# Gathering the tokens of eight experts at once instead of four, in a one-core diffusion step with a mixture of experts

## The reference, cut to what matters

```python
hid = silu(einsum('nd,edf->nef', xt, w_gate)) * einsum('nd,edf->nef', xt, w_up)   # D = 1024, F = 512
hid = hid * gates[..., None]                                                       # zero but for 2 of 16 experts
y = einsum('nef,efd->nd', hid, w_down)
```

## Time and profile before

| | |
|---|---|
| median of 3 runs | 787.18 us (785.57 to 787.45) |
| profiled execution, its time | 786.11 us |
| its span in the trace | 784.2 us |
| TensorE busy | 759.6 us, 97% of the span |
| VectorE, ScalarE, GpSimd busy | 356.6, 160.4 and 58.2 us |
| granted TensorE clock, mean | 0.995 of full speed |
| read from HBM | 286.31 MB, 368 GB/s over the span |

### The profile page before, as it was taken

One profiled execution on the slowest core, in us unless ns is written; L12 is line 12 of the kernel. 1 busy time (PEld: TensorE's weight loads), 2 busy tenths in 40 slices (PEclk: granted clock), 3 DMA queues, 4 the chain that ended last, 5 costly groups with the idle time before them and its releaser, 6 DMA issues.

```text
span 784.2 us, 11547 instructions
## 1 busy us (share of the span) xinstructions
PE 759.6 (97%) x4960; PEld 410.0 (52%) x4967; DVE 356.6 (45%) x560; ACT 160.4 (20%) x368; POOL 58.2 (7%) x70
## 2 busy tenths in 40 slices
PE   6999999999999999999899999999999999999987
PEld 5655646886434443444245546788643444344424
DVE  0206899786422232132248956788732223213222
ACT  3111224504112111120021111460411211112002
POOL 0410052001100000000010005200110000000000
PEclk8999999999999999999999999999999999999999
DMA  8999699898999999999999970679979999999993
GB/s 313 369 357 409 237 386 410 315 390 327 426 409 427 426 419 424 424 420 425 421 398 401 387 287 8 250 286 393 387 303 399 427 426 419 424 427 417 425 421 148
DMA packets 52980, 289.45 MB, mean 369 GB/s; under 512 B 3448, under 2 KB 5808, under 8 KB 27840
## 3 DMA queue, kind: packets, MB, share of 16 engines
q1 hardware_dynamic: 51200, 285.30, 90.4%
q0 software_dynamic: 1488, 3.31, 1.3%
q10 hardware_dynamic: 240, 0.08, 0.0%
HBM read 286.31 MB, written 2.37 MB: 368 GB/s over the span
## 4 chain that ended last, share of the span: by engine, by line
PE 77%; DMA 12%; DVE 5%; SPq 3%; issue 2%; ACT 1%; POOL 0%; DVEq 0%; ACTq 0%
PE ps L1236 23%; PE ps L879 12%; PE ps L1266 12%; PE ps L1150 7%; DMA ring<-in_w_e_up 5%; PE ps L1220 4%; DMA ring<-in_w_e_down 4%; DMA ring<-in_w_mod 3%; PE ps L897 3%; PE ps L1281 2%; SPq L635 1%; PE ps L727 1%; DVE pT L1860 1%; PE ps L1248 1%; PE ps L1028 1%
## 5 line engine op out<-in xcount | busy, mean ns | idle before, releaser
L1236 PE MATMUL ps<-ring,xe 128*64 128x512 f32 x688 | 151.6, 594 | 4.2 <-DMA ring<-in_w_e_up 4.2
L879 PE MATMUL ps<-ring,hT 128*128 128x512 f32 (+1 forms) x320 | 125.7, 551 | 0.0
L1236 PEld LDWEIGHTS ps<-ring,xe 128*64 128x64 f32 x688 | 48.6, 137 | 105.1 <-issue 100.6
L2205 DVE COPY ye<-ps 64x512 f32<-64x512 f32 (+1 forms) x28 | 19.3, 689 | 163.7 <-PE ps L1266 163.5
L1266 PE MATMUL ps<-ring,exhid 128*32 128x512 f32 x736 | 92.3, 594 | 0.8 <-DMA ring<-in_w_e_down 0.6
L879 PEld LDWEIGHTS ps<-ring,hT 128*128 128x128 f32 x320 | 60.1, 190 | 60.7 <-issue 58.4
L1150 PE MATMUL ps<-hT,ring 128*128 128x256 f32 x256 | 57.1, 381 | 0.0
L2189 DVE RECIPROCAL exhid<-exhid 128x512 f32<-128x512 f32 x16 | 53.6, 3353 | 0.5
L2187 DVE TENSOR_SCALAR exhid<-exhid 128x512 f32<-128x512 f32 x16 | 6.8, 427 | 103.2 <-ACT exhid L1678 103.2
L1266 PEld LDWEIGHTS ps<-ring,exhid 128*32 128x32 f32 x736 | 26.0, 110 | 53.0 <-issue 49.4
L1150 PEld LDWEIGHTS ps<-hT,ring 128*128 128x128 f32 x256 | 48.0, 190 | 7.4 <-issue 1.0
(11 more groups left out here) (294 smaller groups left out, 867.0 us busy)
## 6 DMA issues: line engine op xcount, KB each, us to landing
ring<-in_w_mod SPq DMA_DIRECT2D x24, 2048.0 KB, 16.8
ring<-in_w_e_up SPq DMA_DIRECT2D x23, 2048.0 KB, 19.9
ring<-in_w_e_gate SPq DMA_DIRECT2D x20, 2048.0 KB, 22.8
ring<-in_w_e_down SPq DMA_DIRECT2D x19, 2048.0 KB, 23.1
beside<-in_w_e_gate SPq DMA_DIRECT2D x8, 2048.0 KB, 22.1
ring<-in_w_in SPq DMA_DIRECT2D x7, 2048.0 KB, 20.4
beside<-in_w_e_down SPq DMA_DIRECT2D x7, 2048.0 KB, 20.3
beside<-in_w_e_up SPq DMA_DIRECT2D x5, 2048.0 KB, 18.6
```

What stands on the lines that cost most here:

```text
L879: mm = pe.matmul(bank[:, 0:width], hT[:, k, b * P:(b + 1) * P], w[:, k, :], start=(k == 0), stop=(k == KD - 1))
L1236: mm = pe.matmul(bank[PLACES * j:PLACES * j + PLACES, :], xe[:, k, c:c + PLACES], w[:, j, i, :], start=(k == 0), stop=(k == KD - 1))
L2205: ins = dve.tensor_copy(ye[r, plane, 512:1024], bank[r, :])
```

## The change

The tokens of eight experts are gathered at once, with 256 columns per product, ahead of pair 0 and inside pair 3. There is a second place for gathered tokens: `xe` holds the first four experts of a half, and a new tile `small` the other four. `small` is shared with the mixer's small tiles, so ScalarE and VectorE wait for the stores of the state before they write it, and the columns of ones are written again in each layer. A bank now holds one block of 128 features for eight experts, and is copied out by two instructions, on ScalarE for even blocks and on VectorE for odd ones. `count` moves to bank 6.

```diff
@@ bank_plan
-        put(("count", l), 5)
-        for i, bank in enumerate((0, 3, 1, 2)):
-            put((("gather", 0, i), l), bank)
+        for k in range(KD):
+            put((("gather", 0, k), l), (0, 3, 4, 5)[k % 4])
+        put(("count", l), 6)
...
-            if pair % 2 == 1 and pair < PAIRS - 1:
-                for i in range(4):
-                    put((("gather", pair // 2 + 1, i), l), i % 2)
+            if pair == PAIRS // 2 - 1:
+                for k in range(KD):
+                    put((("gather", 1, k), l), k % 2)
@@ build
-        C0 = sb("C0", [P, 2 * MH, MD + 1])
...
+        small = sb("small", [P, KD * 4 * PLACES])
...
+        C0 = share(2 * MH * (MD + 1)).rearrange("p (g e) -> p g e", g=2 * MH)
...
+        places = (xe, small[:, :].rearrange("p (k c) -> p k c", k=KD))
@@ TensorE
-                def gather(q, *which):
-
-                    for i in which:
-                        bank = begin((("gather", q, i), l))
-                        for k in range(2):
-                            for b in range(NB):
-                                c = b * TOK + k * P
-                                mm = pe.matmul(bank[:, c:c + P], htok[:, b, 2 * i + k, :],
-                                               pick[:, b, 4 * q:4 * q + 4, :].rearrange("p e c -> p (e c)"), start=True, stop=True)
-                        done((("gather", q, i), l), mm)
+                def gather(h, *which):
+
+                    for k in which:
+                        bank = begin((("gather", h, k), l))
+                        for b in range(NB):
+                            mm = pe.matmul(bank[:, b * 2 * P:(b + 1) * 2 * P], htok[:, b, k, :],
+                                           pick[:, b, 8 * h:8 * h + 8, :].rearrange("p e c -> p (e c)"), start=True, stop=True)
+                        done((("gather", h, k), l), mm)
...
-                    refill = p % 2 == 1 and q + 1 < QUADS
+                    refill = p == PAIRS // 2 - 1
...
-                        gather(q + 1, 0, 1)
+                        gather(1, 0, 1, 2, 3)
                     turn_hidden(p)
...
-                        gather(q + 1, 2, 3)
+                        gather(1, 4, 5, 6, 7)
...
-                gather(0, 0, 1, 2, 3)
+                gather(0, *range(KD))
@@ ScalarE
+                def pick_out(h, *which):
+
+                    for k in which:
+                        key = (("gather", h, k), l)
+                        bank = full(act, key)[:, :].rearrange("p (b q e s) -> p q b e s", b=NB, q=2, e=4)
+                        for q in range(2):
+                            ins = act.activation(places[q][:, k, :].rearrange("p (e b s) -> p b e s", e=4, b=NB), bank[:, q], ACT.Copy)
+                        ins.then_inc(free(key), 1)
...
-                pick_out(0, 0, 1, 2, 3)
+                act.wait_ge(state_out, 16 * STATE_OUTS * (l + 1))
+                pick_out(0, 0, 2, 4, 6)
@@ VectorE
-            dve.memset(vx[:, :, :, HD:], 1.0)
-            dve.memset(cv[:, :, HD:], 1.0)
...
                 normalise(l)
                 dve.memset(mv[:, :, :, MD:MD + 1], 1.0)
+                dve.memset(vx[:, :, :, HD:], 1.0)
+                dve.memset(cv[:, :, HD:], 1.0)
...
-                chosen(0, 4).then_inc(pick_ready, 1)
+                chosen(0, 8).then_inc(pick_ready, 1)
...
-                chosen(4, E).then_inc(pick_ready, 1)
+                chosen(8, E).then_inc(pick_ready, 1)
...
+                dve.wait_ge(state_out, 16 * STATE_OUTS * (l + 1))
+                pick_out(0, 1, 3, 5, 7)
                 modulation_columns(*last_section(l))
...
+                    if refill:
+                        pick_out(1, 1, 3, 5, 7)
```

More of the change, by code:

```diff
@@ L318, in build, with share @@
         m0 = sb("m0", [64, DEPTH, NB])
-        C0 = sb("C0", [P, 2 * MH, MD + 1])
[L320 to L326, removed]
+        small = sb("small", [P, KD * 4 * PLACES])
+        took = [0]
+        def share(n):
+            took[0] += n
+            return small[:, took[0] - n:took[0]]
+        C0 = share(2 * MH * (MD + 1)).rearrange("p (g e) -> p g e", g=2 * MH)
+        ck = share(NKV * HD)
+        cv = share(NKV * (HD + 1)).rearrange("p (g d) -> p g d", g=NKV)
+        vx = share(NB * NKV * (HD + 1)).rearrange("p (b g d) -> p b g d", b=NB, g=NKV)
+        rstd = share(TOK)
+        qc = share(NB * 4 * 8).rearrange("p (b q g) -> p b q g", b=NB, q=4)
+        qk_r = share(NB * (NQ + NKV)).rearrange("p (b h) -> p b h", b=NB)
+        peaks = share(NB * NQ).rearrange("p (b h) -> p b h", b=NB)
+        hr = share(NB * MH).rearrange("p (b h) -> p b h", b=NB)
+        nst = share(P)[0:8, :]
         shares = sb("shares", [P, NB, NQ])
         dn = sb("dn", [P, NB, MH, 2])
-        hr = sb("hr", [P, NB, MH])
-        nst = sb("nst", [8, P])
         mnew = sb("mnew", [64, DEPTH])
@@ L1210, in _ @@
                 token_rows(3)
-                warm((("scat", 0), l), 3)
-                def gather(q, *which):
-                    for i in which:
-                        bank = begin((("gather", q, i), l))
-                        for k in range(2):
-                            for b in range(NB):
-                                c = b * TOK + k * P
-                                mm = pe.matmul(bank[:, c:c + P], htok[:, b, 2 * i + k, :],
-                                               pick[:, b, 4 * q:4 * q + 4, :].rearrange("p e c -> p (e c)"), start=True, stop=True)
-                        done((("gather", q, i), l), mm)
+                warm((("gather", 0, 2), l), 3)
+                def gather(h, *which):
[5 more added lines that the diff above has]
+                        done((("gather", h, k), l), mm)
                 def into_hidden(p, u):
@@ L1231, in into_hidden @@
                             k = KD // 2 * part + i
-                            if p % 2 == 0 and u == 0 and k % 2 == 0:
-                                taken(pe, (("gather", p // 2, k // 2), l))
+                            if p % 4 == 0 and u == 0:
+                                taken(pe, (("gather", p // 4, k), l))
                             for j in range(2):
                                 c = (p % 2 * 2 + j) * PLACES
-                                mm = pe.matmul(bank[PLACES * j:PLACES * j + PLACES, :], xe[:, k, c:c + PLACES], w[:, j, i, :],
+                                mm = pe.matmul(bank[PLACES * j:PLACES * j + PLACES, :], places[p // 2 % 2][:, k, c:c + PLACES], w[:, j, i, :],
                                                start=(k == 0), stop=(k == KD - 1))
@@ L1665, in _ @@
                 token_copy(3)
[L1667 to L1672, removed]
+                def pick_out(h, *which):
[5 more added lines that the diff above has]
+                        ins.then_inc(free(key), 1)
                 def pair(p):
-                    q, a = p // 2, p % 2
-                    refill = a == 1 and q + 1 < QUADS
+                    refill = p == PAIRS // 2 - 1
                     bank = full(act, (("gate", p), l))
@@ L1684, in pair @@
                     if refill:
-                        pick_out(q + 1, 0, 1)
+                        pick_out(1, 0, 2)
                     key = (("turn", p), l)
@@ L1689, in pair @@
                     if refill:
-                        pick_out(q + 1, 2, 3)
+                        pick_out(1, 4, 6)
                     key = (("down", p, 0), l)
@@ L2176, in _, with pick_out @@
                 dve.tensor_tensor(beb(R_G), beb(R_W), per_col(r(R_X, 6, 8), E), ALU.mult).then_inc(gates_ready, 1)
+                def pick_out(h, *which):
+                    for k in which:
+                        key = (("gather", h, k), l)
+                        bank = full(dve, key)[:, :].rearrange("p (b q e s) -> p q b e s", b=NB, q=2, e=4)
+                        for q in range(2):
+                            ins = dve.tensor_copy(places[q][:, k, :].rearrange("p (e b s) -> p b e s", e=4, b=NB), bank[:, q])
+                        ins.then_inc(free(key), 1)
+                dve.wait_ge(state_out, 16 * STATE_OUTS * (l + 1))
+                pick_out(0, 1, 3, 5, 7)
                 modulation_columns(*last_section(l))
```

## The result

The kernel after takes 795.63 us (median of 4 runs, 795.25 to 796.65), the kernel before 787.09 us in the same comparison: 1.0114 times as long, 95% interval 1.0097 to 1.0132. The forecast was 793.1 us in a range from 789.5 to 796.5 us: slower, as said, but by 2.5 us more, and above the forecast's own range of 791.3 to 794.9 us. By the medians the change costs 8.5 us. The profiled execution took 795.25 us with a span of 793.3 us, 9.1 us more than before.

The account below looks back on a forecast made before the run. The prediction took the weight stream, held back by the first gather, as the bound. Two layers at +3.25 us took the profiled 786.11 us to 792.6; adjusted for run spread, 793.1 us, own range 791.3 to 794.9, with rivals 789.5 to 796.5.

Parts of the forecast that it names:

- Reading of the profile: Expert stages: the gapless weight stream behind the first gather sets their end, at 422 and 420 GB/s, despite TensorE's 97%.
- First gather: Ahead of pair 0 in each layer: 16 products of 256 columns take 7.06 us for 3.81, so 3.25 us more.
- rival that prices a product by the instruction: First gather: wide instructions cost 119 ns like narrow ones, so it stays 3.81 us; no change, 786.6 us; 6%.
- It passes on in full: From first gather to stage end: the whole 3.25 us delay reaches the end of each layer, 2 x 3.25 = +6.5 us.
- Layer 0: Transfers have some stock at 204.88 us, none at 225.38 us; the 0.3 us gap there grows by 3.25 us.
- rival by which layer 0 hides the delay: Queue at 225.38 us holds more, so layer 0's stream ends as before, +0.9 us there; 790.8 us; 10%.
- Copies: Two per bank on ScalarE and VectorE, 1.77 us per bank against 2.65 us available: they fit and cost nothing.
- `chosen`: Ahead of the gather: eight experts take about 0.2 us more, covered by ScalarE's last copy; cost nothing, uncovered 0.2 us per layer.
- waits for the state: New `state_out` waits of ScalarE and VectorE ahead of pair 0: already over when reached, because GpSimd passes the same wait; nothing.
- late banks: Rival at the first gather: PSUM banks come back late, 1.1 us more per layer, 795.3 us; 8%.
- Pairs 1 and 5: A gather vanishes from each: some 1.8 us saved of 3.8, the rest becoming TensorE waits for VectorE and ScalarE.
- rival that TensorE's total sets the end: Expert stages: two gathers of 7.06 us replace four of about 3.8, 1.0 us less per layer; 784.5 us; 6%.

Follow-up runs that it names:

- third experiment: Changed kernel with only four experts gathered ahead of pair 0, the next four in pair 1, 32 unused products in pair 5: 786.52 us, 0.9991 of the kernel before.
- fourth experiment: Kernel before plus four extra 512-column products between `count` and the first expert product, in each layer: 795.24 us, ratio 1.0106.
- first experiment: Changed kernel plus 64 unused 16-column products per layer (128 instructions) where TensorE waits in pairs 1 and 5: 793.6 us, 1.0078 of the kernel before.
- fifth experiment: Changed kernel plus 64 unused products (128 instructions) at the very front: 791.95 us, 1.0064 of the kernel before.
- second: Kernel before plus 64 unused 16-column products (128 instructions) at the front, where TensorE waits for its first weights: 790.0 us, ratio 1.0038.
- sixth experiment: Kernel before plus 128 unused products (256 instructions) at the front: 788.29 us, ratio 1.0023.
- seventh experiment: Changed kernel with only two experts gathered ahead of pair 0, two in pair 0, four in pair 1, the rest wide in pair 3: 791.7 us, 1.0065 of before.
- eighth experiment: Changed kernel with the same two-expert first gather, and `count` moved behind the first expert product: 792.52 us, 1.0067 of the kernel before.

## Why the prediction was right, and where it was not

**Reading of the profile.** Right: TensorE's 97% said nothing, the stream of weights behind the first gather did. The third and fourth experiments are the two halves of the proof: take the growth away and the time is back, add only a delay and the time is lost. The waits for weights that are left in pair 7 of the kernel after, and those of the fourth experiment, say that it is the stream and not TensorE's sum.

**First gather.** 3.25 us more were forecast, 7.14 - 3.81 = 3.33 and 7.15 - 3.81 = 3.34 us measured; the price by rows 7 held. The rival that prices a product by the instruction is refuted at 256 columns: there the rows, and not the figures of the Trainium skill (TensorE: Matmul & The Clock Gate, Back-to-back issue gap), decide. At 64 and 128 columns, though, the seventh experiment shows a price by the instruction, 118 ns for 64 columns and 119 ns for 128.

**It passes on in full.** That was somewhat too much. Stages of the three kernels with the wide first gather (after, first and fifth experiment) are longer than before by 2.42, 3.07, 3.12 us in layer 0 and 2.09, 2.83, 2.40 us in layer 1, a mean of 2.66. Stages of the kernels whose first gather is as before (second, third and sixth experiment) differ from it by -0.96 to +0.33 us, a mean of -0.36; such is the scatter of one profile each. So some 2.7 to 3.0 us of 3.33 arrive per layer, 5.3 to 6.0 us for the forecast's 6.5. By the clock, the first and fifth experiments are 5.4 to 6.8 us slower than the kernel before on the same chip, the fifth with a 0.65 us stall at its end. What takes the rest up is open, but for a part of layer 1: there the last down product waited 0.61 us for its weights in the kernel before, and in the kernel after it does not.

**Layer 0.** The sum was right, its place was not. The prediction gave the queue some stock at 204.88 us and put the growth at 225.38 us. The windows show the larger hole at 208 to 212 us, right behind the late first issue, and a smaller one at 230 to 232. The rival by which layer 0 hides the delay has fallen with it.

**Copies, `chosen`, waits for the state, banks.** Costed at nothing, and the third experiment, which leaves the shared memory and ScalarE's wait in, agrees; VectorE's copies and its wait are judged by the start of the first expert product alone. In the kernel after the first expert product starts 0.35 us (`count`) after the gather's end, and the 32 instructions of the gather take 7.14 us for the 7.06 of the earlier trace rows; late banks are not to be seen.

**Pairs 1 and 5.** Right. From the up product's end (242.86 us) to the down product 2.41 us, where it was about 4.2: 1.8 us saved of 3.8. In the first experiment's pair 1 the 32 unused products fit into the rest without a delay (2.29 us).

**The rival that TensorE's total sets the end**, 784.5 us: refuted for the kernel after. It has 121 records of TensorE fewer, and its stages end later with TensorE waiting for weights in pair 7, 1.23 us at the last block in both layers. But the margin is thin: in the seventh and eighth experiments TensorE's own sum does reach the end.

**The missing term.** The step that failed is the sum: it let the change act only through its work, and had no term for where the code lies. In the trace the stall and the lower clock behind it lengthen the step into layer 1 by 4.37 us. By the clock, counted from the kernel before in each comparison, moving the code at the front (fifth experiment) takes off 3.1 us (8.5 less 5.4), and that kernel still has its own stall of 0.65 us at the end; the first experiment takes off 1.7 us (8.5 less 6.8), where the intervals of the ratios reach 1.4 us (after) and 1.8 us to either side. So 5.3 to 6.0 us of gather and about 2 to 4 us of stall make up the 8.5 us, and the forecast of 6.5 us came close to the first and had nothing for the second. That the range held the time is luck: it reached so high for the late banks (795.3 us), which turned out to cost nothing.

## What to carry to other kernels

Look for the wait at which a full buffer is first given back: work ahead of the first product that reads such a buffer is paid nearly in full (2.7 to 3.0 of 3.33 us per layer here). The same work later is free only as long as the engine still waits for transfers at the end, 2.1 and 2.7 us here, and these waits are soon used up. Widening a product saves little where its price goes by the column (223 ns for 256 columns, 119 ns for 128) and narrowing it nothing where it goes by the instruction (118 ns for 64 columns), so measure both ends in the kernel's own trace. When a kernel's time moves by some us that no wait explains, look for "issue" gaps behind branches, and move the code (here by 128 instructions) before the change is blamed.

## What was not expected of the hardware

**Code that comes late.** A shift of 128 instructions made TensorE stand still for 3.60 and 3.64 us at the end of layer 0, and for 0.65 and 0.91 us at the end of layer 1; a shift of 256 did not. In the trace of the kernel after, the list of DMA queues from 401 to 406.5 us has no packet on the queue named "instruction". From 406.5 to 408.5 us, within the stall, it has one:

```profile
q8 instruction: 1, 0.02, 3.2%
```

In the kernel before, a packet of the kind passes from 398 to 401 us, ahead of the branch, and none from 401 to 405 us:

```profile
q8 instruction: 1, 0.02, 2.3%
```

The profile does not say whose instructions this queue brings. Its 40 packets over the kernel after are about as many as TensorE's 9,678 products and weight loads would fill at 256 to a packet (38, an estimate from the counts and the period in the table).

The reading, which is not shown: behind the branch lies a piece of code that is not there yet when TensorE jumps to it, if it lies in another block than the one last loaded. That it is this branch is argued from where the gap stands and was not tried by itself. In the two short gaps at the end of layer 1 (second and fifth experiments) no packet of the kind passes, and the last one before each passes more than 1 us ahead of the gap; for them the reading rests on the shift alone. The Trainium skill (Advanced Engine Details and Errata, ISA Cache) gives instruction memory in lines of 16 KB, 256 instructions; the period in the table agrees. That section gives no time for a load of code that is missing; the gaps here are 0.65 to 3.64 us long. Why it is 3.6 us at one place and under 1 us at the other is open: the transfers run at 414 GB/s during the former.

**The clock behind it.** The granted clock was 1.00 in the stall, during which TensorE did nothing, and then 0.70 and 0.50 in the windows behind it. The same four products (L802) take 1.82 us at 412.33 us, on the lower level, and 0.87 us at 415.62. That is the part of the 4.37 us that is not the stall itself.
